# Three buffers instead of six for the high halves of the weights, and three gate units loaded before the experts

## What is computed

```
for i in range(DEPTH):                                 # DEPTH = 2
    u = rms_norm(h, attn_norm_g[i]) @ w_in[i]
    ...                                                # conv module | SSD | latent attention on parts of u
    h = h + concatenate([y_conv, y_ssd, y_mla]) @ w_out[i]
    hn = rms_norm(h, ffn_norm_g[i])
    if i % 2 == 0:
        h = h + swiglu(hn, dense_w_gate, dense_w_up, dense_w_down)
    else:
        h = h + moe_top2(hn, router, wg, wu, wd)       # 8 experts, 1024 x 3584, top 2
    gate = sigmoid(rms_norm(h, ple_norm_g[i]) @ ple_w_gate[i])
    h = h + (p[i] @ ple_w_proj[i]) * gate
return rms_norm(h, final_norm_g)
```

## Time and profile before

| | |
|---|---|
| median of 3 runs | 1445.52 us (1445.41 to 1447.06) |
| the profiled execution: its own time | 1446.83 us |
| its span (first to last instruction) | 1445.0 us, 18296 instructions |
| PE, PEld busy | 1400.2 us (97%), 1007.5 us (70%) |
| DVE, ACT busy | 859.0 us (59%), 694.8 us (48%) |
| chain that ended last | PE 88%, DVE 6%, DMA 3%, ACT 2% |
| loads of expert weights | 384 units of 896 KB |

### The profile page before, as it was taken

The page is one execution under the profiler, slowest core; times in us unless marked ns, Lnnn a source line. Parts: engine busy times, 40 slices in busy tenths (PEclk is TensorE's granted clock), DMA queues, the critical chain, the costliest instruction groups (busy, mean ns, idle before and its releaser), DMA issues.

```text
span 1445.0 us, 18296 instructions
## 1 busy us (share of the span) xinstructions
PE 1400.2 (97%) x6999; PEld 1007.5 (70%) x6999; DVE 859.0 (59%) x986; ACT 694.8 (48%) x783; POOL 6.9 (0%) x14
## 2 busy tenths in 40 slices
PE   7999999999989999999999999999999999999996
PEld 6878888888887787766666666666666666666535
DVE  6996645553579978555554556454656555656425
ACT  6566543542555657354444444444444444444315
POOL 0000000000000000000000000000000000000000
PEclk9999999999999999999999999999999999999998
DMA  9415555555543019999999999999999999999992
GB/s 330 160 62 171 186 192 177 193 183 199 170 140 123 9 40 420 377 420 419 399 408 419 406 419 418 389 415 413 409 419 419 396 412 417 406 419 419 419 410 84
DMA packets 99669, 443.89 MB, mean 307 GB/s; under 512 B 7728, under 2 KB 22096, under 8 KB 99328
## 3 DMA queue, kind: packets, MB, share of 16 engines
q1 hardware_dynamic: 98688, 439.30, 77.9%
q0 software_dynamic: 896, 3.44, 0.6%
HBM read 440.61 MB, written 2.10 MB: 306 GB/s over the span
## 4 chain that ended last, share of the span: by engine, by line
PE 88%; DVE 6%; DMA 3%; ACT 2%; issue 1%; DVEq 0%; ACTq 0%; SPq 0%
PE psum L629 20%; PE psum L630 19%; PE psum L631 19%; PE psum L1146 13%; PE psum L1160 7%; DMA ring<-in_moe_w_down 2%; PE psum L674 2%; PE psum L1058 1%; PE psum L692 1%; PE psum L652 1%; DVE arena_a L2069 1%; PE psum L1175 1%; DMA ring<-in_moe_w_up 1%; PE psum L1183 1%; DVE arena_a L2206 1%
## 5 line engine op out<-in xcount | busy, mean ns | idle before, releaser
L1982 DVE TENSOR_TENSOR ring_lo<-ring,w_hi 128x1792 fp32r<-128x1792 f32 x191 | 385.5, 2024 | 264.5 <-ACT w_hi L1475 262.5
L1475 ACT ACTIVATE w_hi<-ring 128x1792 fp32r<-128x1792 f32 x191 | 322.9, 1700 | 253.0 <-DMA ring<-in_moe_w_up 109.6
L631 PE MATMUL psum<-w_hi,hidden_b 128*128 128x512 f32 x624 | 230.2, 369 | 0.0
L1976 DVE TENSOR_TENSOR ring_lo<-ring,w_hi 128x2048 fp32r<-128x2048 f32 (+1 forms) x68 | 152.6, 2266 | 102.8 <-ACT w_hi L1469 102.7
L1146 PE MATMUL psum<-ring,xT 128*64 128x512 f32 (+1 forms) x1024 | 206.6, 545 | 0.0
L629 PE MATMUL psum<-w_hi,hidden_b 128*128 128x512 f32 (+1 forms) x512 | 192.6, 376 | 4.8 <-ACT arena_b L1779 3.0
L630 PE MATMUL psum<-ring_lo,hidden_b 128*128 128x512 f32 (+1 forms) x512 | 188.0, 367 | 0.0
L629 PE MATMUL psum<-w_hi,xT_parts 128*128 128x512 f32 (+1 forms) x384 | 150.4, 392 | 4.0 <-DVE xT_parts L1993 3.4
L629 PE MATMUL psum<-w_hi,hidden_a 128*128 128x512 f32 (+1 forms) x384 | 148.3, 386 | 2.7 <-DVE ring_lo L1982 2.3
L631 PE MATMUL psum<-w_hi,xT_parts 128*128 128x512 f32 (+1 forms) x384 | 149.1, 388 | 0.0
L630 PE MATMUL psum<-ring_lo,xT_parts 128*128 128x512 f32 (+1 forms) x384 | 149.1, 388 | 0.0
(11 more groups left out here) (333 smaller groups left out, 1449.7 us busy)
## 6 DMA issues: line engine op xcount, KB each, us to landing
ring<-in_moe_w_gate SPq DMA_DIRECT2D x128, 896.0 KB, 7.5
ring<-in_moe_w_up SPq DMA_DIRECT2D x128, 896.0 KB, 8.5
ring<-in_moe_w_down SPq DMA_DIRECT2D x128, 896.0 KB, 8.3
ring<-in_w_in SPq DMA_DIRECT2D x16, 1024.0 KB, 5.7
ring<-in_dense_w_gate SPq DMA_DIRECT2D x14, 1024.0 KB, 5.1
ring<-in_dense_w_up SPq DMA_DIRECT2D x14, 1024.0 KB, 5.1
ring<-in_dense_w_down SPq DMA_DIRECT2D x14, 1024.0 KB, 4.9
ring<-in_w_out SPq DMA_DIRECT2D x8, 1024.0 KB, 4.8
```

The costliest lines, as they stand in the source:

```text
L631: return mm(o, a[1], b[0], start=False, stop=final)
L1475: A(heavy_high(c), moe_raw(m), ACT.Copy).then_inc(hi_ready, 1)
L1976: V.tensor_tensor(low(g, sizes[g]), raw(g, sizes[g]), f32(high(g, sizes[g])), ALU.subtract).then_inc(lo_ready, 1)
L1982: V.tensor_tensor(moe_low(m), moe_raw(m), f32(heavy_high(c)), ALU.subtract).then_inc(lo_ready, 1)
```

## The change

From the last output projection (`w_out` of the second layer, turn `S1`) on, the high parts go round in buffers 0 to 2 of `w_hi` alone (`M_HIGHS` = 3). Buffers 3 to 5 are then free: the raw gate units 0 to 2 of the last stage are loaded into them (as `w_raw`, the same memory), right after the last load ahead of the experts. They are split after the last heavy unit: high parts into buffers 0 to 2, low parts over the raw bytes in 3 to 5. The fourth gate unit still goes through the ring, and its high part into ring slot 0.

```diff
+M_HIGHS = 3
...
-        w_hi = sb("w_hi", HIGHS * UNIT, F32R)
+        w_raw, w_hi = shared("w_raw", HIGHS * UNIT, "w_hi", HIGHS * UNIT)
...
+        S1 = TURN[FRONT1 + 10]
+        def slot_of_turn(t):
+            return t % HIGHS if t < S1 else (t - S1) % M_HIGHS
+        def unit_before(t):
+            if t >= S1 + M_HIGHS:
+                return t - M_HIGHS
+            return max((b for b in range(min(t, S1)) if b % HIGHS == slot_of_turn(t)), default=None)
...
         def heavy_high(c):
-            a = (S0 + c) % HIGHS * UNIT
+            a = slot_of_turn(S0 + c) * UNIT
...
+        EARLY = HIGHS - M_HIGHS
         def after_raw(c):
-            return ring[:, c * UNIT:(c + 1) * UNIT]
+            return w_raw[:, (M_HIGHS + c) * UNIT:(M_HIGHS + c + 1) * UNIT] if c < EARLY else ring[:, c * UNIT:(c + 1) * UNIT]
         def after_low(c):
-            return ring_lo[:, c * UNIT:(c + 1) * UNIT]
+            return w_hi[:, (M_HIGHS + c) * UNIT:(M_HIGHS + c + 1) * UNIT] if c < EARLY else ring_lo[:, c * UNIT:(c + 1) * UNIT]
+        def after_high(c):
+            return w_hi[:, c * UNIT:(c + 1) * UNIT] if c < EARLY else ring_lo[:, 0:UNIT]
...
         def high_reader(i, c):
-            if c >= HIGHS:
-                return heavy_reader(i, c - HIGHS)
+            if c >= M_HIGHS:
+                return heavy_reader(i, c - M_HIGHS)
...
+            sp.wait_ge(*last_reader[PARTED[S1 - 1]])
+            for c in range(EARLY):
+                load_after(c)
             sp.wait_ge(flag_ready, 1)
...
-            for c, (src, k, n) in enumerate(after_moe):
+            for c in range(EARLY, len(after_moe)):
...
                         heavy_y_parts(i)
+                        for c in range(EARLY):
+                            after_split(i + 1, c)
                         take_light_y(i, 2)
-                        after_split(i + 1, 0)
                     def after_split(n, c):
                         act.wait_ge(ple_in[c], 16)
-                        act.wait_ge(*high_reader(n, c))
-                        A(high(N0 + c), after_raw(c), ACT.Copy).then_inc(hi_ready, 1)
+                        act.wait_ge(d_full, d_done(n - 1, 1))
+                        A(after_high(c), after_raw(c), ACT.Copy).then_inc(hi_ready, 1)
...
                     for half in range(2):
                         take_xT(3 * L + 2, L, "g_ple", (2 * half, 2 * half + 1))
-                        after_split(n_iter, 1 + half)
...
                     for n in range(4):
                         add_back(i, 0, n, LAST_SCATTER[n])
+                    for c in range(EARLY):
+                        after_split(i + 1, c)
                     light_y_rest(i, 2)
```

More of the change, by code:

```diff
@@ L107 @@
 LATER = M_DOWNS
-assert PAIR_UNITS % M_SLOTS == 0 and M_UNITS % HIGHS == 0 and LATER % M_SLOTS == 0
+assert PAIR_UNITS % M_SLOTS == 0 and M_UNITS % M_HIGHS == 0 and LATER % M_SLOTS == 0
 HEAVY_FILLS = tuple((ch, t, min(4, 2 * RUN - t)) for ch in range(NCH) for t in range(0, 2 * RUN, 4))
@@ L566, in high @@
         def high(g, n=UNIT):
-            a = turn(g) % HIGHS * UNIT
+            a = slot_of_turn(turn(g)) * UNIT
             return w_hi[:, a:a + n]
         def heavy_high(c):
-            a = (S0 + c) % HIGHS * UNIT
+            a = slot_of_turn(S0 + c) * UNIT
             return w_hi[:, a:a + CHUNK]
@@ L1286, in after_unit @@
                 pe.wait_ge(lo_ready, turn_of(n_iter, c) + 1)
-                return tuple(b.rearrange("p (k n) -> p k n", k=k) for b in (high(N0 + c), after_low(c)))
+                return tuple(b.rearrange("p (k n) -> p k n", k=k) for b in (after_high(c), after_low(c)))
             def last_x(half):
@@ L1355, in high_reader @@
         def high_reader(i, c):
-            if c >= HIGHS:
-                return heavy_reader(i, c - HIGHS)
+            if c >= M_HIGHS:
+                return heavy_reader(i, c - M_HIGHS)
             if isinstance(i, int) and i == 0:
-                return last_reader[PARTED[S0 + c - HIGHS]]
-            return heavy_reader(i - 1, M_UNITS + c - HIGHS)
+                return last_reader[PARTED[unit_before(S0 + c)]]
+            return heavy_reader(i - 1, M_UNITS + c - M_HIGHS)
         @block.sync
@@ L1378, in moe_load, with load_after @@
                 sp.dma_start(moe_raw(m).rearrange("p (k n) -> p k n", k=1), src).then_inc(mloaded[m % M_SLOTS], 16)
+            def load_after(c):
+                src, k, n = after_moe[c]
+                sp.dma_start(after_raw(c).rearrange("p (k n) -> p k n", k=k), src).then_inc(ple_in[c], 16)
+            sp.wait_ge(*last_reader[PARTED[S1 - 1]])
+            for c in range(EARLY):
+                load_after(c)
             sp.wait_ge(flag_ready, 1)
@@ L1414, in _ @@
                 moe_load(j - M_DOWNS, expert_unit(*last, DOWN0 + j))
-            for c, (src, k, n) in enumerate(after_moe):
+            for c in range(EARLY, len(after_moe)):
                 covered = ((c + 1) * UNIT - 1) // CHUNK
                 sp.wait_ge(*light_reader(n_iter - 1, M_UNITS - M_SLOTS + covered))
-                sp.dma_start(after_raw(c).rearrange("p (k n) -> p k n", k=k), src).then_inc(ple_in[c], 16)
+                load_after(c)
             sp.wait_ge(ysb_ready, d_done(n_iter - 1, 1))
@@ L1466, in split @@
                 act.wait_ge(loaded[g % SLOTS], landed(g))
-                if turn(g) >= HIGHS:
-                    act.wait_ge(*last_reader[PARTED[turn(g) - HIGHS]])
+                before = unit_before(turn(g))
+                if before is not None:
+                    act.wait_ge(*last_reader[PARTED[before]])
                 A(high(g, sizes[g]), raw(g, sizes[g]), ACT.Copy).then_inc(hi_ready, 1)
@@ L1986, in after_split @@
                 dve.wait_ge(hi_ready, turn_of(n, c) + 1)
-                V.tensor_tensor(after_low(c), after_raw(c), f32(high(N0 + c)), ALU.subtract).then_inc(lo_ready, 1)
+                V.tensor_tensor(after_low(c), after_raw(c), f32(after_high(c)), ALU.subtract).then_inc(lo_ready, 1)
             def rest(lo, exact, hi, gain=None):
@@ L2595, in experts @@
                     add_back(n_iter - 1, 1, n, LAST_SCATTER[n])
-                after_split(n_iter, 0)
                 return n_iter
```

## The result

| | before | after |
|---|---|---|
| median of the 14 runs of each | 1445.92 us (1444.71 to 1447.63) | 1448.53 us (1445.15 to 1453.13) |
| ratio, 95% interval | | 1.0018 (1.0010 to 1.0027) |
| the profiled execution: time, span | 1446.83, 1445.0 us | 1447.84, 1446.0 us |

The changed kernel is 2.6 us slower (1.4 to 3.9 by the interval). That is 0.18%, inside the 0.2% that the prediction called no change, but the interval leaves 1.0 out, so the loss is real. The forecast was +0.5 us.

What follows compares the result with a forecast made beforehand. PE bounds the chain (88%), in step with the experts' 419 GB/s stream. 1446.83 + 2.43 at the start - 1.93 at the end = 1447.3 us profiled, 1446.0 us as a median; 8-in-10 range 1442.6 to 1449.0 us.

Steps and rivals of the forecast that it cites:

- no change: Whole kernel: a difference within about 0.2%, 2.9 us, of the kernel before, between 1442.6 and 1448.4 us; chance 0.68.
- rival 2: Start of the experts: longer PE stops each bring another 3.4 us at 1.2 GHz, 1447.7 to 1449.4 us; 17%.
- The end, 1.93 us: Before the first gate matmul: DVE goes to `take_xT` without a low part in between, gaining 1.93 us.
- The start, 2.43 us of stops: Heavy units 8 and 16: `silu` and `gated` queue behind waiting splits, costing 1.09 and 1.34 us.
- This delay stays.: From heavy unit 16 on: the 2.43 us delay is passed on through PE's release and the back-to-back stream.
- what PE loses behind unit 16 can be taken up by 644.87, since PE only follows the stream there: Experts behind heavy unit 16: argument against up to 2 x 1.7 us of added lower-clock loss.
- more stretches near 595: Sign of being wrong: more stretches at clock 0.50 near 570 or 595 in the new profile.
- the likeliest case: Start cost and end gain, both on the chain, cancel: 1444.6 to 1448.0 us; 60%.
- The sentence on the clock rule: Start: longer stops bring one more 3.4 us stretch at half speed, median near 1447.7 us instead of 1446.0.
- Price 0 for the experts after the start, for the last output projection and for the early loads: There, new waits end before data arrives or with 1.0 us to spare, and early loads change nothing: 0 us.

Runs made afterwards that it cites:

- one split back: Changed kernel with the third gate split returned to the end, on DVE between the last add-back and `take_xT`: 1450.82 us, ratio 1.0027.
- mended kernel: Changed kernel with the first `silu` ahead of heavy unit 10's split and the first `gated` ahead of unit 17's low part: 1441.61 us, ratio 0.9975.
- the same order in the kernel before: Kernel before, six buffers and old end, with the first `silu` and first `gated` moved ahead of the splits' work: 1443.72 us, ratio 0.9983.
- the wait alone: Kernel before, with only the experts' heavy splits waiting for PE's read three turns back instead of six: 1450.56 us, ratio 1.0035.
- Four turns back: Kernel before, with only the experts' heavy splits waiting for PE's read four turns back instead of six: 1446.47 us, ratio 1.0003.
- each half of the mended order: Changed kernel with only the first `silu` moved ahead (1443.93 us, 0.9993), or only the first `gated` (1445.55 us, 0.9996).
- `gated` first: Changed kernel with only DVE's first `gated` moved ahead of the low part of heavy unit 17: 1445.55 us, ratio 0.9996.
- the end filled: Changed kernel with matmuls nobody reads (2, 2 and 5) in PE's stops at the end alone: 1447.79 us, ratio 1.0012.
- early table: Mended kernel plus a one-column dummy Silu on ACT behind heavy unit 4's split, loading the table early: 1441.47 us, ratio 0.9968.

## Why the prediction was right, and where it was off

The forecast of no change and the range held: 1448.53 us lies within 1442.6 to 1449.0, near its upper end. But the sum behind them, 1446.0 us, left out a part of the cost, and the range held only because it had room for most of rival 2. By its steps:

- **The end, 1.93 us.** Right. The changed kernel shows 1.91 us (5.96 against the forecast 5.94 from ACT's copy to the first product), and taking one split back gave the same 1.91 us again. In whole times it is less sure: 1.2 us (mended kernel against the same order in the kernel before), 1.3 us (one split back) and 2.5 us (the wait alone against the changed kernel) by the ratios. All three have the right sign, but only the last is clear of the intervals, and only just.
- **The start, 2.43 us of stops.** The mechanism was right, place by place: the two stops grew by 1.15 and 1.32 us, together 2.47, forecast 1.09 and 1.34. At unit 16 1.79 us had arrived: 0.45 us had been won before unit 7, and the stretch at 1.2 GHz behind unit 8 cost 0.2 us less than before. Four turns back, and each half of the mended order, confirm what stands behind what.
- **"This delay stays."** Right. Less the offset, the changed kernel is 3.0 us late at the first light matmuls behind unit 17 and between 3.0 and 3.9 us from there to the last pair.
- **The bound of the start: rival 2.** This is the term that was mis-sized: the sum had nothing for more lower clock at the start. I had put the clock behind unit 16 aside with "what PE loses behind unit 16 can be taken up by 644.87, since PE only follows the stream there". A new stretch at 1.2 GHz came (more stretches near 595 were among the signs of being wrong that I had named), and 1.2 us of it had arrived at the DMA of 648.64, the one I thought would take it up. Why it did is argued, not shown: PE's reads release the slots, so loads behind unit 16 are issued later by what PE loses. Filling the stops without shortening them took 3.5 us off. With one more stretch the sum is 0.5 + 1.7 = 2.2 us, against 2.6 measured. The profile of the changed kernel may understate this: of the five with an unfilled stop of 4.17 us it is the only one with a single stretch behind it.
- **The forecast of rival 2**, 1447.7 to 1449.4 us, is where the time came out; the likeliest case, 1444.6 to 1448.0, ended 0.5 us short of it. The sentence on the clock rule said near 1447.7 us. By that rule of the Trainium skill ("TensorE: Matmul & The Clock Gate", "Why this matters for your kernels": avoid idle gaps between bursts of matmuls), the trace agrees: the stop of 2.59 us before unit 16 was followed by a stretch at 0.50 in each of the six kernels that had it unfilled. The gap that the page still allows is longer than this stop; here the measurement decides.
- **Price 0 for the experts after the start, for the last output projection and for the early loads.** Nothing speaks against it, though no run has the early loads alone. The wait alone, without early loads, is no faster than the changed kernel, and PE's waits from 595 to 1370 us for low parts came to 3.2 us in four pieces, where they were 2.3 us in three:

```profile
PE psum L648 <- DVE ring_lo L2009: 3.2, 4, 1.0
```

  The fourth piece, in order of time, has no counterpart in the kernel before:

```profile
1368.51 0.50 PE L648 MATMUL psum<-w_hi,hidden_a 128*128 128x512 f32 x1 [1.03 <-DVE ring_lo L2009]
```

  Between the light rows' matmuls and ACT's last copy the changed kernel lost 4.12 us (4.90 less the offset). Of these, 3.00 were there at the first light matmuls and 3.87 behind the load of 648.64; 3.01 were left in front of this last wait for a low part, and 4.12 behind it. Its chain goes back to a load that took 10.72 us to land, from 1353.88. These two steps of 0.9 and 1.1 us don't come with three buffers as such: the three-turn wait and the mended kernel have neither. The one with the early table has both, which is most of why it took 861.7 us from the light rows' matmuls to the transposes at the end where the mended one took 859.7, though its stop is the shorter one. Why a load lands later in one execution than in another stays open, and a single execution doesn't tell at this size.

## What to carry to other kernels

When a buffer ring gets shallower, don't only ask whether the data still comes in time: list what stands behind each newly waiting instruction on its own engine, in order. Here one more turn of depth, or two pieces of code in another order, decided between 5 us lost and nothing. Price a stop of PE with the clock behind it as well, and pass that loss on if PE's reads release the transfers that bound it later. Where a stop can't be removed, matmuls that nobody reads can keep the clock: 14 and 9 of them did at the start.

## What the runs showed of the hardware that was not expected

- The same stop isn't followed by the same clock in every execution. Behind 4.17 us of idleness came one stretch of 3.4 us at 0.50 in the changed kernel and two in the other four profiles with such a stop (the three-turn wait, one split back, `gated` first, the end filled). The runs of the changed kernel reach from 1445.15 to 1453.13 us with mean clocks of 0.992 down to 0.985, and the longest among them have the low clocks: 1452.03 and 1453.13 us at 0.987 and 0.985, 1445.15 us at 0.992.
- Before units 8 and 16 a stop of 1.10 to 1.76 us was followed by a lower clock in no profile, one of 2.59 us or more in all in which it wasn't filled. Shorter stops aren't safe everywhere. Among the short bursts at the end, with stops of 0.3 to 1.5 us between them, the clock fell in six of seven profiles. Behind a stop of 0.80 us ahead of the light rows' matmuls it fell in two of fourteen, and that cost PE 2.4 us by the end of unit 7.
- The table load took 1.28 us and began before PE's signal for the first `silu` had come (563.84 against 564.43 in the mended kernel), so it cost only the 0.69 us that it stuck out.
